# A new order for the setup of a fused two-block kernel: token-wise first norm, angles on GpSimd, modulation tiles held, two feature tiles first

## What is computed

```python
c_act = jax.nn.silu(c)
mod = c_act @ ada_w[l] + ada_b[l]                      # 1024 x 6144 weights
sh1, sc1, g1, sh2, sc2, g2 = split(mod, 6)
h = rms_norm(x, norm1_g[l]) * (1.0 + sc1) + sh1
proj = h @ w_in[l] + b_in[l]                           # q, k, v, gb, gc, xs
q = rope(q, positions); k = rope(k, positions)         # cos/sin(position * inv_freq)
```

## Time and profile before

| | us |
|---|---|
| median of 3 runs | 1999.88 |
| the three runs | 2000.92, 1998.45, 1999.88 |
| profiled execution, its own time | 1995.88 |
| its span, first to last instruction | 1994.1 |
| TensorE busy (share of the span) | 1940.5 (97%) |
| VectorE, ScalarE, GpSimd busy | 1041.4, 798.0, 173.5 |
| mean granted TensorE clock | 0.993 of full speed |

### The profile page before, as it was taken

One profiled execution on the slowest core, in us unless ns is written; L12 is line 12 of the kernel. 1 busy time (PEld: TensorE's weight loads), 2 busy tenths in 40 slices (PEclk: granted clock), 3 DMA queues, 4 the chain that ended last, 5 costly groups with the idle time before them and its releaser, 6 DMA issues.

```text
span 1994.1 us, 35178 instructions
## 1 busy us (share of the span) xinstructions
PE 1940.5 (97%) x14503; PEld 1576.1 (79%) x14503; DVE 1041.4 (52%) x1509; ACT 798.0 (40%) x1217; POOL 173.5 (9%) x191
## 2 busy tenths in 40 slices
PE   6999999999999999999999999999999999999999
PEld 5777778888887687787778788888868887888887
DVE  6788765555324755778845534432265465343312
ACT  4345243333224545777634332322245353223222
POOL 1100000000014000000001111111100001111010
PEclk8999999999999999999999999999999999999999
DMA  9545223333323132000012233333222223333331
GB/s 320 180 137 148 85 74 95 95 97 114 107 84 82 57 97 84 11 12 8 8 58 75 85 101 98 95 116 101 58 74 80 88 82 89 95 96 106 108 102 43
DMA packets 313904, 181.60 MB, mean 91 GB/s; under 512 B 18717, under 2 KB 306611, under 8 KB 313780
## 3 DMA queue, kind: packets, MB, share of 16 engines
q1 hardware_dynamic: 308354, 162.82, 27.4%
q0 software_dynamic: 4608, 16.78, 2.7%
q10 hardware_dynamic: 818, 0.21, 0.0%
HBM read 177.69 MB, written 2.10 MB: 90 GB/s over the span
## 4 chain that ended last, share of the span: by engine, by line
PE 86%; DVE 6%; ACT 4%; issue 3%; ACTq 1%; POOL 0%; DVEq 0%; POOLq 0%
PE bank L261 23%; PE bank L263 23%; PE bank L262 23%; PE bank L2409 4%; DVE wlo L246 1%; PE bank L1333 1%; PE bank L1335 1%; PE bank L612 1%; PE bank L1334 1%; PE bank L2939 1%; PE bank L3046 1%; ACT whi L239 0%; ACTq L807 0%; PE bank L2944 0%; PE bank L2963 0%
## 5 line engine op out<-in xcount | busy, mean ns | idle before, releaser
L246 DVE TENSOR_TENSOR wlo<-raw,whi 128x1024 fp32r<-128x1024 f32 (+1 forms) x251 | 327.4, 1304 | 644.4 <-ACT whi L239 644.4
L239 ACT ACTIVATE whi<-raw 128x1024 fp32r<-128x1024 f32 (+1 forms) x251 | 280.6, 1119 | 636.6 <-PE bank L263 630.1
L261 PE MATMUL bank<-fh_hi,whi 128*128 128x512 f32 x991 | 387.6, 391 | 5.0 <-DVE wlo L246 3.5
L262 PE MATMUL bank<-fh_lo,whi 128*128 128x512 f32 x991 | 386.3, 390 | 0.0
L263 PE MATMUL bank<-fh_hi,wlo 128*128 128x512 f32 x991 | 386.1, 390 | 0.0
L261 PEld LDWEIGHTS bank<-fh_hi,whi 128*128 128x128 f32 x991 | 186.3, 188 | 46.0 <-DVE wlo L246 4.6
L263 PEld LDWEIGHTS bank<-fh_hi,wlo 128*128 128x128 f32 x991 | 186.4, 188 | 39.1
L262 PEld LDWEIGHTS bank<-fh_lo,whi 128*128 128x128 f32 x991 | 186.4, 188 | 39.1 <-issue 0.5
L261 PE MATMUL bank<-f_hi,whi 128*128 128x512 f32 x528 | 205.7, 390 | 0.0
L263 PE MATMUL bank<-f_hi,wlo 128*128 128x512 f32 x528 | 205.4, 389 | 0.0
L262 PE MATMUL bank<-f_lo,whi 128*128 128x512 f32 x528 | 205.4, 389 | 0.0
(11 more groups left out here) (522 smaller groups left out, 3172.5 us busy)
## 6 DMA issues: line engine op xcount, KB each, us to landing
raw<-in_w_up_dram SPq DMA_DIRECT2D x44, 512.0 KB, 3.7
raw<-in_ffn_w_gate_dram SPq DMA_DIRECT2D x44, 512.0 KB, 3.7
raw<-in_ffn_w_up_dram SPq DMA_DIRECT2D x44, 512.0 KB, 3.7
raw<-in_ffn_w_down_dram SPq DMA_DIRECT2D x32, 704.0 KB, 4.0
late<-in_ada_w_dram POOLq DMA_DIRECT2D x32, 512.0 KB, 4.1
raw<-in_rwkv_w_rkv_dram SPq DMA_DIRECT2D x24, 512.0 KB, 3.4
raw<-in_w_down_dram SPq DMA_DIRECT2D x16, 704.0 KB, 4.0
early<-in_ada_w_dram SPq DMA_DIRECT2D x16, 512.0 KB, 14.0
```

The lines of the kernel that those rows point to most:

```text
L239: act.activation(halves_of(at)[0][:, 0:kts * P], raw_unit(at, kts), ACT.Copy).then_inc(hi_ready, 1)
L246: dve.tensor_tensor(lo[:, 0:kts * P], raw_unit(at, kts), hi[:, 0:kts * P].bitcast(F32), ALU.subtract)\
L261: pe.matmul(dst, hi, rhs_hi(k), start=first and k == 0, stop=False)
L262: pe.matmul(dst, hi, rhs_lo(k), start=False, stop=False)
```

## The change

- **First norm by tokens.** `FirstNorm` replaces `LeadNorm` for the first norm. ScalarE squares the four token-major tiles of `x_tok`, 128 tokens by 1024 features each, with an accumulated row sum (output into the idle `whi` and `wlo`), after all eight copies. Root and reciprocal then act on 128x4 values. TensorE spreads the result over the partitions with four matmuls against the identity into bank 4, where `Split` reads it. The eight sums between the transposes and the reciprocal of 128x512 are gone.
- **Angles on GpSimd.** VectorE keeps the product of position and frequency. `pool_angles` does the rest in 20 chained steps: each fused multiply-add is a multiply and an add.
- **Modulation.** Block 5 moves from TensorE to VectorE. Sums of feature tiles 0 and 1 go to bank 7, those of 2 to 7 to bank 1, and `early_mod` makes modulation and gain for the two tiles first and for the other six after the first weight split.
- **Splits inside the norm.** ScalarE writes `whi` of the first two units ahead of its tiles 1 and 3, VectorE `wlo` ahead of its tiles 2 and 4. The first product starts with hi by hi and hi by lo as soon as `h_hi` of tile 0 is there.
- **Late tiles held.** `pool_late` waits for both splits, not for the transposes.

```diff
@@ -651,6 +657,36 @@
             dve.reciprocal(tok_rstd, tok_std).then_inc(rstd_ready.sem, 1)
             dve.wait_ge(spread_done.sem, self.spread0 + 1)
 
+
+    class FirstNorm(Norm):
+
+
+        def __init__(self):
+            self.sq0 = sq_ready.claim(NT)
+            self.std0, self.rstd0, self.spread0 = std_ready.claim(1), rstd_ready.claim(1), spread_done.claim(1)
+            self.sums, self.rstd = eps_col[:, 28:28 + NT], bank[NORM_BANK][:, :]
+
+        def act_square(self, act, t):
+            act.activation((whi, wlo)[t % 2][:, t // 2, 0:D], x_tok[:, t, :], ACT.Square,
+                           accum_out=self.sums[:, t:t + 1]).then_inc(sq_ready.sem, 1)
+
+        def act_root(self, act):
+            act.wait_ge(sq_ready.sem, self.sq0 + NT)
+            act.activation(tok_std, self.sums, ACT.Sqrt, bias=eps_col[:, 0:1], scale=1.0 / D).then_inc(std_ready.sem, 1)
+
+        def dve_reciprocal(self, dve):
+            dve.wait_ge(std_ready.sem, self.std0 + 1)
+            dve.reciprocal(tok_rstd, tok_std).then_inc(rstd_ready.sem, 1)
+
+        def pe_spread(self, pe):
+            pe.wait_ge(rstd_ready.sem, self.rstd0 + 1)
+            for t in range(NT):
+                mm = pe.matmul(bank[NORM_BANK][:, t * P:(t + 1) * P], tok_rstd[:, t:t + 1].to_broadcast([P, P]),
+                               ident[:, :], start=True, stop=True)
+            mm.then_inc(spread_done.sem, 1)
+
+        def dve_rstd(self, dve):
+            dve.wait_ge(spread_done.sem, self.spread0 + 1)
 
     w_in, w_o, ada_w = (A[n].rearrange("a k n -> (a k) n") for n in ("w_in", "w_o", "ada_w"))
     N_IN, N_O = 18, KD
...
@@ -687,7 +723,7 @@
         more = (at.c // RAW + 1) - (len(seq) + RAW - 1 - at.raw_slot) // RAW
         return slot_count[at.raw_slot] + more * 16 + at.i * (at.step // RAW * 16)
 
-    ON_PE = (2, 5, KD + 1)
+    ON_PE = (2, KD + 1)
     BY_DVE = [m for m in range(EARLY) if m not in ON_PE]
 
     def ada_used(m):
@@ -724,7 +760,7 @@
 
 
     def pool_late(pool):
-        pool.wait_ge(x_turned, KD)
+        pool.wait_ge(lo_ready, 2)
         for n in range(EARLY, 6 * KD):
             if n >= EARLY + RAW:
                 pool.wait_ge(*ada_used(n - RAW))
             tr.then_inc(x_turned, 1)
-            if k >= 2:
-                norm1.pe_sum_of(pe, k - 2)
-        for k in range(KD - 2, KD):
-            norm1.pe_sum_of(pe, k)
         pe.wait_ge(vec_landed, 16 * len(VEC_PLAN))
         for b in range(VB):
             m = P if b < VB - 1 else LAST_ROWS
...
     def act_setup(act):
+        act.wait_ge(const_ready, MORE_CONSTS)
+        act.wait_ge(x_landed, 16 * NT)
         for k in range(KD):
             act.wait_ge(x_turned, k + 1)
             act.activation(x[:, k, :], bank[k % 2][:, :], ACT.Copy).then_inc(x_ready.sem, 1)
-            if k:
-                norm1.act_square(act, k - 1)
-        norm1.act_square(act, KD - 1)
+        for t in range(NT):
+            norm1.act_square(act, t)
         act.wait_ge(small_turned, VEC_TURNED)
         act.activation(vecs[:, 0:n_vec], bank[5][:, 0:n_vec], ACT.Copy).then_inc(vecs_ready, 1)
 
-
-        steps = [0]
+        dve.tensor_scalar(ang[0], bank[2][:, 0:P], invf[:, 0:1], None, ALU.mult).then_inc(angle, 1)
+
+    def pool_angles(pool):
+        pool.wait_ge(angle, 3)
+        steps = [3]
 
         def step(ins):
             ins.then_inc(angle, 1)
             steps[0] += 1
-            dve.wait_ge(angle, steps[0] + 2)
+            pool.wait_ge(angle, steps[0])
 
         a = lambda n: ang[n]
-        step(dve.tensor_scalar(a(0), bank[2][:, 0:P], invf[:, 0:1], None, ALU.mult))
         for n, quarter, shift, dst in ((1, 0.0, 0.0, a(4)), (2, 0.25, float(np.pi / 2), a(5))):
-            step(dve.tensor_scalar(a(n), a(0), 1 / TWO_PI, quarter, ALU.mult, ALU.add))
-            step(dve.tensor_scalar(a(3), a(n), ROUND, ROUND, ALU.add, ALU.subtract))
-            step(dve.scalar_tensor_tensor(a(n), a(3), -TURN1, a(0), ALU.mult, ALU.add))
-            step(dve.scalar_tensor_tensor(dst, a(3), -TURN2, a(n), ALU.mult, ALU.add))
-            step(dve.scalar_tensor_tensor(a(n), a(3), -TURN3, dst, ALU.mult, ALU.add))
-            step(dve.tensor_scalar(a(3), a(n), shift, 3.1415925, ALU.add, ALU.min))
-            step(dve.tensor_scalar(dst, a(3), -3.1415925, None, ALU.max))
-
-    ANGLES = 17
+            step(pool.tensor_scalar(a(n), a(0), 1 / TWO_PI, quarter, ALU.mult, ALU.add))
+            step(pool.tensor_scalar(a(3), a(n), ROUND, ROUND, ALU.add, ALU.subtract))
+            for turn, from_, to in ((TURN1, a(0), a(n)), (TURN2, a(n), dst), (TURN3, dst, a(n))):
+                step(pool.tensor_scalar(a(6), a(3), -turn, None, ALU.mult))
+                step(pool.tensor_tensor(to, a(6), from_, ALU.add))
+            step(pool.tensor_scalar(a(3), a(n), shift, 3.1415925, ALU.add, ALU.min))
+            step(pool.tensor_scalar(dst, a(3), -3.1415925, None, ALU.max))
+
+    ANGLES = 3 + 2 * 10
...
 
     ada_evac, gain_ready = sem("ada_evac"), count("gain_ready")
     ada_sum = sem("ada_sum")
...
         acc, c_ = ada_acc[:, part % 2, :], cact[:, k:k + 1]
         if k == 0:
-            dve.wait_ge(ada_sum, part - 1)
...
+    def early_column(part, n):
+
+        return bank[EARLY_BANKS[n >= EARLY_SPLIT]][:, part * KD + n:part * KD + n + 1]
+
...
     def pe_early_sums(pe, part):
 
         pe.wait_ge(ada_done, len([m for m in BY_DVE if m // KD <= part]))
         for n in range(KD):
-            mm = pe.matmul(bank[ADA_BANKS[0]][:, part * KD + n:part * KD + n + 1],
-                           ada_acc[:, part, n * P:(n + 1) * P], ones[:, 0:1], start=False,
-                           stop=part == 1 and n == KD - 1)
-        mm.then_inc(ada_sum, 1)
+            mm = pe.matmul(early_column(part, n), ada_acc[:, part, n * P:(n + 1) * P], ones[:, 0:1], start=False,
+                           stop=part == 1 and n in (EARLY_SPLIT - 1, KD - 1))
+            if n == KD - 1 or part == 1 and n == EARLY_SPLIT - 1:
+                mm.then_inc(ada_sum, 1)
 
     ADA_SPAN = 32
 
...
+    def early_mod(dve, second):
+        dve.wait_ge(ada_sum, 2 + second)
+        if not second:
+            dve.wait_ge(vecs_ready, 1)
+        ks = slice(EARLY_SPLIT, KD) if second else slice(0, EARLY_SPLIT)
+        both = lambda t_: t_.rearrange("p (a k) -> p a k", a=2)[:, :, ks]
+        dve.tensor_tensor(both(mod[:, 0:2 * KD]), both(bank[EARLY_BANKS[second]][:, 0:2 * KD]),
+                          both(vecs[:, col["ada_b"]:col["ada_b"] + 2 * KD]), ALU.add).then_inc(ada_evac, 1)
+        dve.wait_ge(ada_evac, 1 + second)
+        dve.scalar_tensor_tensor(gain[:, ks], mod[:, KD:2 * KD][:, ks], 1.0, vecs[:, col["norm1"]:col["norm1"] + KD][:, ks],
+                                 ALU.add, ALU.mult).then_inc(gain_ready.sem, 1)
+        dve.wait_ge(gain_ready.sem, GAIN0 + 1 + second)
+
+    GAIN0 = gain_ready.claim(2)
+
...
     x_tile = lambda k: x[:, k, :]
-    norm1 = LeadNorm(x_tile, KD, from_start)
+    norm1 = FirstNorm()
     split1 = Split(x_tile, KD, lambda k: gain[:, k:k + 1], mod_col(0), lambda k: h_hi[:, k, :],
-                   lambda k: h_lo[:, k, :], lambda eng: None)
+                   lambda k: h_lo[:, k, :], lambda eng: None, rstd_=norm1.rstd)
     N_PRE = 6
     prj_ready, rot_done, rope_done = sem("prj_ready"), sem("rot_done"), sem("rope_done")
...
     def pe_mixer1(pe):
-        for m in ON_PE[:2]:
+        for m in ON_PE:
             pe_early(pe, m)
+        norm1.pe_spread(pe)
+        pe_spread(pe)
         pe_early_sums(pe, 0)
-        for m in ON_PE[2:]:
-            pe_early(pe, m)
-        pe_spread(pe)
         pe_early_sums(pe, 1)
         two_units(pe, [at_in[u] for u in range(2)], KD, (bank[0][:, :], bank[1][:, :]), lambda k: h_hi[:, k, :], lambda k: h_lo[:, k, :],
-                  split1.pe_ready(pe))
+                  split1.pe_ready(pe), hi_there=split1.pe_hi_there(pe))
         for u in range(1, N_PRE):
             if u >= 2:
                 pe_in(pe, u)
@@ -1338,10 +1389,8 @@
     def act_mixer1(act):
         norm1.act_root(act)
         act_angles(act)
-        split_hi(act, first[0])
-        split_hi(act, first[1])
         act_spread(act)
-        split1.act(act)
+        split1.act(act, ((1, lambda act: split_hi(act, first[0])), (3, lambda act: split_hi(act, first[1]))))
         for u in range(N_PRE):
             act_in(act, u)
         act.wait_ge(vT_done, 1)
@@ -1374,14 +1423,13 @@
         for n in range(len(BY_DVE)):
             if n == 2:
                 dve_angles(dve)
-            if n == len(BY_DVE) - 3:
-                norm1.dve_rstd(dve)
+            if n == len(BY_DVE) - 4:
+                norm1.dve_reciprocal(dve)
             dve_early(dve, n)
-        split_lo(dve, first[0])
-        split_lo(dve, first[1])
-        ada_add(dve, 0)
-        scaled_gain(dve, "norm1", 1)
-        split1.dve(dve)
+        norm1.dve_rstd(dve)
+        early_mod(dve, 0)
```

(2 more changed lines are left out.)

36 lines of the change are left out of this document (21 added, 15 removed).

## The result

The changed kernel took 2000.89 us in the median of 20 runs, the kernel before 1995.92 in 20 runs beside them: a ratio of 1.0019 (95% interval 1.0011 to 1.0027), so 3.8 us slower (2.2 to 5.4; the two medians alone lie 5.0 apart). The forecast was 3.7 us faster. The three runs shown ahead of the prediction (median 1999.88) lie at the high end of what the kernel before gives, 1992 to 2001. The profiled execution of the changed kernel took 2001.81, its span is 2000.0.

What follows compares the result with a forecast made beforehand. TensorE, busy 97% of the span, bounds the kernel and its matmul stream can only start earlier: S 35.6 plus 19.6 gives E 55.2 against 58.95, 3.7 us less, so 1996.2 for the median 1999.88; range 1992.0 to 2000.5.

Steps and rivals of the forecast that it cites:

- GpSimd's price: Angle chain of 20 steps on GpSimd: 8.5 us from 13.9, done at 22.4, hidden with 6 us to spare.
- Rival (b): GpSimd's angle chain becomes the bound: S moves if it ends after 28.7; time 2016 at the upper row; chance 0.05.
- S: Start of the first normalised tile on VectorE: forecast 35.6 us, 43.30 before, 7.7 us earlier.
- ScalarE, VectorE and TensorE up to S: Setup steps: copies end 21.0, squares 25.4, root about 27.4, VectorE's last blocks 32.9, TensorE's sums 34.8 us.
- the norm's spread: Four 128-column TensorE matmuls spreading the first norm: about 1.1 us at the cold rate, before 29.2, in idle time.
- S to E: First normalised tile to end of first two units: 19.6 us, ends 18.6 and 20.6 by the clock's rise; 15.65 before.
- E: End of the first two weight units, at TensorE's first rotation: forecast 55.2 us against 58.95 before, 3.7 less.
- Rival (a): TensorE's array stays cold through the setup: S 37.2, E 55.8 or 1.1 less gain, time 1996.8 to 1998.8; chance 0.17.
- (c): Rival: VectorE waits for held late tiles landing after 12 us, not 4.1; 2.4 of 3.7 us lost, 1998.6; chance 0.04.
- (d): Rival: holding the late tiles or the early root does nothing; each worth at most 1 us, inside the range.
- Behind E the order is unchanged: After the first two units: same order, transfers released by use, so the 3.7 us saving is carried to the end.

Runs made afterwards that it cites:

- e2: The changed kernel, but VectorE stands still from its second early block until GpSimd's angle chain is done; one time, 1999.46 us.
- e6: e1 with the late tiles not held but issued once the squares are done; ratio to the kernel before 0.9991 (0.9982 to 1.0000).
- e1: The changed kernel with the angle steps back on VectorE, 14 chained steps; ratio to the kernel before 0.9985 (0.9974 to 0.9995).
- e3: The changed kernel with TensorE's angle spread moved behind both modulation sums, angles still on GpSimd; ratio to the kernel before 0.9977 (0.9968 to 0.9986).
- e4: The changed kernel with angles back on VectorE and their spread behind both sums; ratio to the kernel before 0.9986 (0.9975 to 0.9996).
- e7: The changed kernel with each early VectorE row block made in two instructions of 512 columns; ratio to the kernel before 1.0000 (0.9991 to 1.0010).
- e10: e3 with 12 tiny, never-read matmuls added in TensorE's setup; ratio to the kernel before 0.9958 (0.9944 to 0.9971).
- r_after: The changed kernel once more with no edit, for its spread; one time, 1998.20 us.
- e9: The changed kernel with 12 tiny, never-read matmuls added in TensorE's setup; ratio to the kernel before 0.9995 (0.9984 to 1.0006).
- e8: The kernel before, in its old order, with only the angle steps moved to GpSimd; ratio to it 0.9997 (0.9988 to 1.0006).

## Why the prediction was wrong

- *GpSimd's price: the step that failed.* "The columns are those of the lower row, so I take it": 8.5 us for the chain, done at 22.4. It took 21.0 and was done at 34.7. Alone it takes 11.8 (e2), so 3.3 us of the error are the size of a step and 9.2 are the company of VectorE, of which the prediction had no term. Rival (b) was the case, GpSimd as the bound, and in size, though it has no word of VectorE's company: its own rule (S moves by what the chain ends after 28.7) gives 35.6 + 6.0 = 41.6, and 41.39 was measured. It had a chance of 0.05, since the bounds 0.31 and 1.75 were read as prices of an engine left alone.
- *ScalarE, VectorE and TensorE up to S.* Copies to 21.8 for 21.0, squares to 25.9 for 25.4, root done 28.0 for 27.4, last row block 33.6 for 32.9, both sums 6.99 for 7.0. One term was mis-sized and misplaced: the norm's spread, "about 1.1 at the cold rate ... in time in which TensorE has nothing else", took 2.08 and ended at 30.8 (e6), so S at the rate assumed is 36.84, not 35.6. The 35.0 to 35.8 of e1, e3, e4, e7 and e10 are no confirmation: in e1 and e7 the clock was back during the sums, in e3, e4 and e10 the angles' spread stands behind them. Without GpSimd's chain and with a late clock the gain would have been some 1.2 us smaller than forecast.
- *S to E.* The two ends, 18.6 and 20.6, are both seen: 18.5 in e1 and e3, 20.6 in the changed kernel, 20.5 in r_after. The first product came at S + 3.83 for 3.95, the last lower half at S + 14.1 for 14.4 (the prediction's own terms add up to 14.2, and those of S to 35.5).
- *Rival (a)* was the case as far as the transposes go, hidden behind GpSimd's chain. All 32 ran at 1.2 GHz in the changed kernel (0.42 us each), where the prediction had tiles 5 to 7 in the warm array, and its own reading of the slow first rows was right. They end at 21.2 (22.0 in (a)), the root is done at 28.0 (28.7), and where nothing waits for GpSimd the norm's spread ends at 30.8 (31.1) and S is 36.84 (37.2; its terms add up to 37.4): e6. But the array didn't stay cold: the clock rose at 21.1 and fell at 24.5. What the prediction quotes, that transposes do not engage the full clock, is not borne out: in e3 the clock rose at 20.2, with nothing but transposes on TensorE since 17.0, and the last of them took 0.27.
- *(c)* was not the case, no tile was late. *(d)* held for the late tiles (e6); the early root has no run of its own.
- *"Behind E the order is unchanged ... so the saving is carried to the end."* Half wrong. The order is, the place in the program is not, and that costs 3.0 us in the RWKV stage (e9: 1.0019 to 0.9995). Over the whole way it is 1.7 (means of three traces each, 1935.4 for 1933.7): behind the stage the three traces of before have five falls of the clock and those of the changed kernel two, which no run explains. Together, 1.7 in the setup and 1.7 in the way make 3.4 of the 3.8 measured.
- *The base.* The one trace of before had an early clock and an E of 58.95; three traces give 60.2. A forecast made against one execution carries that scatter of up to 3 us. The median of three, 1999.88, was 4.0 above that of 20; it is luck that 2000.89 comes within 0.4 us of the range's end.

## What to carry to other kernels

An engine that is idle is not free: before work is put on GpSimd, look at what VectorE runs at the time, and price a step by VectorE's instruction beside it, not by its own columns. Put what depends on a slow side chain behind whatever does not, in each engine's program; e3 bought 8 us with two moved calls. And when a kernel is a long stream of small instructions on one engine, compare the idle times without a cause far behind the edit: a change of a few instructions moves them.

## What the runs showed of the hardware beyond that

- A GpSimd step on 128x128 takes 0.29 to 0.67 us alone and up to 1.50 beside VectorE's two-input blocks of 1.3 (1.83 once in e8); VectorE itself loses 0.1 us (five blocks in 6.96 with it, 6.85 in e1 without).
- Moving 12 matmuls of TensorE's program is worth 2 to 3 us some 900 us later, by stops of up to 1.5 us each at the ends of pieces of 126.7 matmul records; a stop can bring a fall of the clock for 3.4 us with it, worth 1.2 us more.
- TensorE begins at 1.2 GHz: in all 18 traces its transposes take 0.42 us until the clock's record begins, at 19.1 to 22.1 us, and 0.27 after it. A clock column of 1.00 ahead of the first record says nothing.
- The granted clock fell at 24.5 us in the changed kernel (23.5 and 25.5 in its other traces), for 31.9 to 33.5 before, when the transposes were through and only thin sums ran; in e1 it was back at 32.2, in the sums, for 3.4 us.
